# Expert weights loaded in halves of 2 MB into three places, instead of quarters of 1 MB into six

## What is computed

```python
xb = h_pad[tok]
gate = jnp.minimum(xb @ w_gate[e] + b_gate[e], SWIGLU_LIMIT)
up = jnp.clip(xb @ w_up[e] + b_up[e], -SWIGLU_LIMIT, SWIGLU_LIMIT)
return ((up + 1.0) * gate * jax.nn.sigmoid(SWIGLU_ALPHA * gate)) @ w_down[e] + b_down[e]
```

## Time and profile before

| | us |
|---|---|
| median of three runs | 1865.66 |
| lowest and highest | 1864.57, 1866.84 |
| the profiled execution, its own time | 1866.3 |
| its span, first to last instruction | 1864.5 |
| PE busy in the span | 1685.9 |
| DVE busy | 1426.8 |
| ACT busy | 1101.2 |
| mean granted clock of TensorE | 0.943 |

### The profile page before, as it was taken

The page is one execution under the profiler, slowest core; times in us unless marked ns, Lnnn a source line. Parts: engine busy times, 40 slices in busy tenths (PEclk is TensorE's granted clock), DMA queues, the critical chain, the costliest instruction groups (busy, mean ns, idle before and its releaser), DMA issues. The chain is left out here.

```text
span 1864.5 us, 26939 instructions
## 1 busy us (share of the span) xinstructions
PE 1685.9 (90%) x8992; PEld 1315.8 (71%) x8992; DVE 1426.8 (77%) x1336; ACT 1101.2 (59%) x1042; POOL 329.0 (18%) x312
## 2 busy tenths in 40 slices
PE   3999878888779869999999999999999999999982
PEld 2777656555554447888888888888888888888871
DVE  4422464477433758999999999999999999999993
ACT  4221443354322345777777777777777777777762
POOL 0000112300101000231231231231231231231120
PEclk9999878799889769999999999999999999999996
DMA  9454473500135167999999999999999999999973
GB/s 346 165 197 149 85 227 112 176 30 2 29 132 182 68 259 291 355 371 381 373 373 377 377 371 374 382 370 372 384 372 377 379 376 378 380 375 373 381 257 123
DMA packets 112695, 516.42 MB, mean 277 GB/s; under 512 B 25741, under 2 KB 47581, under 8 KB 59898
## 3 DMA queue, kind: packets, MB, share of 16 engines
q1 hardware_dynamic: 99690, 485.84, 69.1%
q0 software_dynamic: 12944, 29.78, 5.9%
HBM read 502.75 MB, written 31.61 MB: 287 GB/s over the span
## 5 line engine op out<-in xcount | busy, mean ns | idle before, releaser
L2730 PE MATMUL banks<-split 128*128 128x512 f32 x4608 | 1078.3, 393 | 7.5 <-DVE split L2895 5.8
L2730 PEld LDWEIGHTS banks<-split 128*128 128x128 f32 x4608 | 861.7, 189 | 193.3 <-issue 13.5
L2891 DVE TENSOR_TENSOR split<-expert_buffers,split 128x2048 fp32r<-128x2048 f32 x384 | 864.4, 2283 | 44.0 <-ACT split L2820 42.5
L2820 ACT ACTIVATE split<-expert_buffers 128x2048 fp32r<-128x2048 f32 x384 | 733.1, 1918 | 221.2 <-PE banks L2730 215.4
L2670 POOL TENSOR_TENSOR expert_buffers<-routing 128x1 f32<-128x1 f32 x63 | 76.2, 1210 | 828.7 <-PE banks L2738 467.1
L2693 POOL DMA_INDIRECT ffn_rows<-expert_buffers x32 | 109.0, 3406 | 5.3 <-issue 5.3
L526 PE MATMUL banks<-w_in_high,hT_high 128*128 128x476 f32 x192 | 75.6, 394 | 4.2 <-DVE hT_low L413 4.2
L2895 DVE TENSOR_TENSOR split<-banks,split 128x1024 fp32r<-128x1024 f32 x64 | 77.7, 1214 | 2.0 <-ACT split L2823 2.0
L439 DVE COPY arena<-banks 128x476 f32<-128x476 f32 x12 | 7.8, 653 | 91.1 <-PE banks L526 91.0
L526 PE MATMUL banks<-w_in_high,hT_low 128*128 128x476 f32 x192 | 73.1, 381 | 0.0
L2823 ACT ACTIVATE split<-banks 128x1024 fp32r<-128x1024 f32 x64 | 64.5, 1008 | 8.8 <-PE banks L2738 8.8
(11 more groups left out here) (377 smaller groups left out, 1674.3 us busy)
## 6 DMA issues: line engine op xcount, KB each, us to landing
expert_buffers<-in_w_gate SPq DMA_DIRECT2D x128, 1024.0 KB, 8.1
expert_buffers<-in_w_up SPq DMA_DIRECT2D x128, 1024.0 KB, 5.8
expert_buffers<-in_w_down SPq DMA_DIRECT2D x128, 1024.0 KB, 8.5
arena<-in_w_ada SPq DMA_DIRECT2D x16, 1024.0 KB, 4.8
w_in_landing<-in_w_in SPq DMA_DIRECT2D x5, 1904.0 KB, 14.1
arena<-in_w_ada SPq DMA_DIRECT2D x4, 2048.0 KB, 20.5
arena<-in_x_prompt SPq DMA_DIRECT2D x8, 512.0 KB, 9.9
arena<-in_cache_cmp POOLq DMA_DIRECT2D x32, 128.0 KB, 3.7
```

The costliest lines, as they stand in the source:

```text
L2730: last = pe.matmul(ps[:, bank + c, :], x[:, kt * P:(kt + 1) * P].bitcast(F32R), wt.bitcast(F32R), start=(m == 2 and kt == 0 and x is xs[0] ...
L2820: act.activation(high[:, j % RING_Q].bitcast(F32R), v, ACT.Copy).then_inc(s_high, 1)
L2891: dve.tensor_tensor(rest[:, j % RING_Q].bitcast(F32R), v, high[:, j % RING_Q], ALU.subtract).then_inc(s_rest, 1)
```

## The change

The six places become three, each of two quarters (the same memory, `core.w`), with one semaphore each. One DMA brings a half of a matrix: 128 partitions x 4096 words, contiguous 16 KB per partition on both sides. SP waits until both quarters that lay in the place are done. ACT waits for the place's semaphore before each of its two quarters; rounding, subtraction and products stay by quarters. The six quarters ahead of the stage become three halves, and up quarters 2 and 3 of the first block become one half.

```diff
--- before.py
+++ after.py
@@ -2124,8 +2124,8 @@
                 sp.dma_start(core.h2_d[t0:t0 + n, :], h2[0:n, t % 2, :]).then_inc(s_h2o[t % 2], 16)
                 if t == ST:
                     sp.wait_ge(s_yp, NT)
-                    for i in range(LANDING):
-                        load_quarter(core, sp, 0, i // 4, i % 4, i)
+                    for i in range(LANDING // 2):
+                        load_half(core, sp, 0, i // 2, i % 2, i)
             for u in range(2):
                 sp.wait_ge(s_h2o[u], 16 * ((NT + 1 - u) // 2))
             for t, (t0, n) in enumerate(TILES):
@@ -2530,13 +2530,13 @@
     core.moe.end = LANDING * QK * D + 5 * D
     core.z_late = core.z_moe + core.moe.end
     mats = [core.io[n].rearrange("a e (p k) n -> (a e) p k n", k=KT) for n in ("w_gate", "w_up", "w_down")]
-    return w, mats, [core.sem(f"w_in{i}", carry=True) for i in range(LANDING)]
-
-
-def load_quarter(core, sp, e, m, q, place):
-
-    sp.dma_start(core.w[:, place, :, :],
-                 core.mats[m][bass.ds(e, 1), :, q * QK:(q + 1) * QK, :].rearrange("e p k n -> (e p) k n")
+    return w, mats, [core.sem(f"w_in{i}", carry=True) for i in range(LANDING // 2)]
+
+
+def load_half(core, sp, e, m, h, place):
+
+    sp.dma_start(core.w[:, 2 * place:2 * place + 2, :, :].rearrange("p s k n -> p (s k) n"),
+                 core.mats[m][bass.ds(e, 1), :, 2 * h * QK:2 * (h + 1) * QK, :].rearrange("e p k n -> (e p) k n")
                  ).then_inc(core.s_w[place], 16)
 
 
@@ -2625,17 +2625,16 @@
 
             def quarters(m, e, prev, c):
 
-                for q in range(4):
-                    sp.wait_ge(s_rest, 12 * prev + c + q + 9 - LANDING)
-                    load_quarter(core, sp, e, m, q, (8 + c + q) % LANDING)
+                for h in range(2):
+                    sp.wait_ge(s_rest, 12 * prev + c + 2 * h + 10 - LANDING)
+                    load_half(core, sp, e, m, h, (8 + c + 2 * h) % LANDING // 2)
 
             e = expert(0)
             biases(0, e, None)
             biases(1, e, None)
 
-            for q in range(2, 4):
-                sp.wait_ge(s_rest, q - 1)
-                load_quarter(core, sp, e, 1, q, q - 2)
+            sp.wait_ge(s_rest, 2)
+            load_half(core, sp, e, 1, 1, 0)
 
             def step(k, prev):
 
@@ -2814,7 +2813,7 @@
             def high_part(j, prev):
 
                 v, quarter, number = landed(j, prev)
-                act.wait_ge(s_w[quarter % LANDING], 16 * (quarter // LANDING + 1) + (0 if prev is None else 32 * prev))
+                act.wait_ge(s_w[quarter % LANDING // 2], 16 * (quarter // LANDING + 1) + (0 if prev is None else 32 * prev))
                 if not (prev is None and j < RING_Q):
                     act.wait_ge(s_used, number - (RING_Q - 1))
                 act.activation(high[:, j % RING_Q].bitcast(F32R), v, ACT.Copy).then_inc(s_high, 1)
```

## The result

The changed kernel takes 1897.11 us (median of four runs, 1892.52 to 1898.85) against 1866.25 us of the kernel before on the same chip: a ratio of 1.0181, 95% interval 1.016 to 1.0203. It is slower by 30.9 us, the difference of the medians. The forecast was slower, 1888, with 1865 to 1912 as the range.

A forecast was written before the change was run, and what follows sets the result against it. PE was taken as the bound, busy all 35.07 us of a step. Lateness of 0.8 us over 30 steps less a 1.3 us cushion adds 22.7 us to 1866.3; 1889, as median 1888, range 1865 to 1912.

The forecast's parts named there:

- Lateness per step: ACT's rounding of down quarter 2 in the expert stage starts 0.8 us late each step, carried on by DVE.
- the 7.4 for the first half: Up's first half, a 2 MB load, lands 7.4 us after its issue; ends 7.2 and 7.6.
- the 0.4 us taken off: Lateness cut from the mean 1.2 us because a bigger first load covers the old queue's wait for a place.
- Part 1: When a load starts: even quarters wait about 2.3 us, one subtraction, for most halves; 5.85 us for up's first half.
- those 5.85 us: Between the ends of down quarters 2 and 3 on DVE, DMA engines have nothing to move for most of the time.
- released by DMA once a step, at down quarter 2: Sign of being right: ACT's rounding waits for a load's landing once per step, at down quarter 2.
- PE idle at gate's first quarters: Sign of being right: PE idles 0.5 to 1.2 us a step there, released by DVE.
- the forecast's last sign: Forecast as a whole is wrong if PE's new idle time stands behind another half than down's second.
- Costed at nothing: Rest of the change, including 192 SP issues instead of 384, bias loads, and start and end of the stage: no cost.
- B: Rival: not slower, down's second half lands in time, lateness 0.12 us per step or less; 1866 us, chance 0.2.
- C: Rival: much slower, longer packets stretch the row store's drain and down loads; lateness 2.0 us, 1925 us, chance 0.12.
- D: Rival: faster, fewer fixed costs in the transfers, gain only from the first two steps; 1862 us, chance 0.04.

The follow-up runs named there:

- e1: Kernel before, with both 1 MB loads of a half issued only when both quarters of the place are done; landing semaphores stay per quarter: 1861.30 us, ratio 1.0001.
- e2: Kernel before, quarters still issued singly, but the two of a half share one semaphore and ACT waits for both: 1863.28 us, ratio 0.9996.
- e3: Kernel before with the edits of e1 and e2 together, each half as two 1 MB loads back to back: 1899.73 us, ratio 1.0194.
- e6: Changed kernel plus one DVE operation of 0.68 us between the activation and the rest of down quarter 3: 1907.97 us, ratio 1.0252.
- e7: Changed kernel plus the same DVE operation as e6, placed behind the rest of up quarter 1: 1893.99 us, ratio 1.0181.
- e10: e3 with up quarter 2 alone issued at its own release: 1886.32 us, ratio 1.0156.
- e4: e3 with up quarter 0 alone issued at its own release: 1902.99 us, ratio 1.0225.
- e9: e3 with up quarters 0 and 2 both issued at their own releases; gate and down keep the late release: 1886.04 us, ratio 1.0141.
- e5: Changed kernel with DVE taking the rest of down quarter 3 before reading the up sum and the activation: 1889.33 us, ratio 1.0152.
- e12: Changed kernel with DVE's activation moved behind the rest of gate quarter 1, loads and waits untouched: 1872.04 us, ratio 1.0075.
- e8: Changed kernel with the accumulating row store replaced by a store of one 4-byte word per partition to scratch: 2030.63 us, ratio 1.0918.

## Why the prediction was right, and where it was not

**Direction and size held, and the mechanism in the main.** PE was the bound and full; two waits together, not one, took its place; and DVE's order carries the lateness on from step to step. e1, e2 and e3 show the second apart from everything else: 0, 0 and all. e6 against e7 shows the third. Which of the late releases matter, the prediction had wrong.

**Lateness per step.** I said 0.8 us. The shown step has 25.56 - 24.81 = 0.75, but it is a short one: the step is 1.01 us longer in the mean of 23. Over the same 23 it is 7.56 us from the issue of up's first half to ACT's up quarter 0, 5.92 on to up quarter 2 and 12.31 on to down quarter 2, 25.79 together, so 0.98 late. 30 x 0.98 - 1.3 = 28 against the measured 30.9. The mis-sized terms: the 7.4 for the first half was good. The second half of up comes 5.92 behind it and not 5.0; e10, which gives that half's first quarter its own release, has 5.23 in the same mean where e3 has 5.93, so most of this is its own late release. The last two halves with the row store take 12.3, where the sum had 10.0 and, from the step of before, 24.4 - 5.7 - 15.0 = 3.7 for the store, 13.7 together. The first of these errors made the forecast too low, the second too high, and the 0.4 us taken off, on the belief that a bigger first load covers a gap in the queue, too low again: the gap behind up's first half got longer, not shorter. That the sum came within a quarter of the truth is in part luck.

**Where the loop runs.** The prediction put the whole loss through the release of down quarter 3 and the first half of up. With the other part of the change in place, giving up's first quarter back its own release changes nothing (e4), and with none of up's releases delayed 26.6 us remain (e9). The late releases of gate's and down's halves, which Part 1 called "one subtraction" each and let pass, are enough for most of the loss. e4, e5, e10 and e12 fit a second way round, nearly equal in length, on which DVE goes on to gate quarter 1 and the queue starts again with up's second half; that it is the only other one is ruled out by e9, and the ways through gate and down were not followed singly.

**An idle queue during those 5.85 us.** Part 1 said that most of that time the DMA engines would have nothing to move. The trace shows otherwise: in the last 5.9 us before that release they are busy 0.90 of the time in the changed kernel, at 346 GB/s:

```profile
1247.30:1253.20 5.90, 5.51 (x25) 4.22 (x23) 5.83 (x6) 4.25 (x3) 1.27 (x3) 1.00 0.90 346
```

Gate's second half was still coming in; it released ACT only at 1254.32. What the release opens is a thin place of two or three us (0.84 and 219 GB/s above), and not a hole of five.

**The share of the DMA engines.** Foreseen as down by two or three hundredths: 0.98 to 0.95.

**ACT "released by DMA once a step, at down quarter 2".** It happens there, but also at four more halves, and the largest totals are those of up and gate. At gate's halves and up's first that costs DVE next to nothing, since it is not yet ready for those quarters. At up's second half it does: DVE idles 1.16 us a step there in the mean of the 23 steps, against 0.46 at down quarter 2. "PE idle at gate's first quarters": the wait stands at down quarter 3, one link earlier (1217.41, 1.70 us), and comes to 0.7 us a step. That is still behind down's second half, as the forecast's last sign asked.

**Costed at nothing:** transfers of 2 MB in place of 1 MB came to nothing within some 6 us (e3). The start and end of the stage were not tried alone.

**Rivals.** B, the last half in time, is what e1 and e2 show, and not the changed kernel. C, a store made dearer by longer packets, falls with e3: packets of 8 KB lose as much. D found nothing to gain.

**The page's formula.** "DMA: Bandwidth & Descriptors" (section "Anatomy of one DMA") of the Trainium skill would put a lone 2 MB at 6.8 us as an estimate. The shortest in the shown step, issue to the release of ACT, is 7.2, and no load of a half in the changed kernel is seen to land sooner. The measurement decides: with 6.8 the sum gave 5 us, a sixth of the loss.

## What to carry to other kernels

When fewer and larger buffers replace smaller ones, follow one buffer round: the wait for its last user, the issue, the whole landing, the user again, and what else that engine does in between. If this sum comes near the step that the busiest engine needs, late release and late landing must be judged together; here each was free and both cost 31 us. Do it for every buffer of the ring, and not only for the one with the longest delay: here giving back the longest delay, 5.85 us, brought nothing by itself (e4). And giving one transfer a head start in this queue, 98% busy before the change, only moved the gap to the next one that was released late.

## What was not expected of the hardware

In e8 GpSimd stores 4 bytes from each of 128 partitions, 0.5 KB a step, in place of the rows. The half of up issued beside it came some 5 us later, in the median of the stretch too. DMA issues between 820 and 1520 us (KB each, median us to landing), of the changed kernel and then of e8, and one step's timeline of e8:

```profile
expert_buffers<-in_w_up SPq DMA_DIRECT2D x40, 2048.0 KB, 7.7
```

```profile
expert_buffers<-in_w_up SPq DMA_DIRECT2D x35, 2048.0 KB, 13.1
...
scratch_rows<-expert_buffers POOLq DMA_DIRECT2D x17, 0.5 KB
```

```profile
1318.24 0.60 POOL L2693 DMA_DIRECT2D scratch_rows<-expert_buffers  x1
...
1331.19 3.71 ACT L2819 ACTIVATE split<-expert_buffers 128x2048 fp32r<-128x2048 f32 x2 [6.84 <-DMA expert_buffers<-in_w_up]
```

The step went to about 41 us (from one end of down quarter 3 to the next, 1271.04 to 1312.71, it is 41.67) and the kernel to 2030.63: half a kilobyte in 4-byte pieces delayed the loads more than the whole accumulating row store does. Why is open: no run changes the size of the pieces alone.
